# Weight tiles as three 256-column matmuls into one PSUM region, without the copy and add of result halves

## The chip, the cores and the metric

The kernel runs on one core of one Trainium2 chip. The metric is the device time of one execution in microseconds (us); lower is better. TensorE is called PE in the profile (PEld is its weight loads), VectorE DVE, ScalarE ACT, GpSimd POOL, SyncE SP.

## The reference, cut to what matters

Two layers over 256 tokens of width 2048, all in float32. Nearly all of the arithmetic is in products of a 256-row activation with a large weight matrix:

```python
for layer in range(2):
    hn = rms_norm(h, mix_norm[layer])
    if layer == 0:   # attention: 2048 -> 2560 (q, k, v), then 2048 -> 2048
        mix = swa_sink_attention(hn, a_w_qkv, a_b_qkv, a_sinks, a_w_o, a_b_o)
    else:            # recurrent block: 2048 -> 4096, gates, scan over time, 2048 -> 2048
        mix = rglru_block(hn, b_w_in, ..., b_w_out, b_b_out)
    h = h + mix
    h = h + jnp.square(jax.nn.relu(rms_norm(h, mlp_norm[layer]) @ w_up)) @ w_down   # 2048 -> 8192 -> 2048
return rms_norm(h, final_norm)
```

## The kernel before, in words

Everything is kept transposed: 128 features on the partitions and 256 tokens (TOK) along a row. To keep float32 accuracy, each operand is split into a rounded high part and the rest: a weight w becomes w_hi and w_lo, an activation becomes a pair stored as `operand[:, 0]` (high) and `operand[:, 1]` (low). A product is then hi·hi + hi·lo + lo·hi.

The weights are streamed in 85 "quads" of 512 output features: 5 for q, k, v; 4 for the attention's output; 32 for each MLP; 8 for the recurrent block's input; 4 for its output. A quad has two halves of 256 output features ("pairs"), a half has four chunks of four 128-row weight blocks, and a chunk has eight weight tiles of 128x128 (two output blocks b, four rows k). So a half has 32 tiles, a quad 64, the kernel 85·64 = 5440. A half writes two PSUM banks, and the two halves of a quad use different ones.

Each engine has its own program with the order of its work written out by hand:

- SP loads each 512 KB chunk into `w_raw`, which has eight slots; a slot is free once DVE has made w_lo from it.
- ACT makes w_hi from each chunk (`split_hi`, L343), as soon as the products of the chunk one half earlier have left that place. At the end of each half, between the third and fourth chunk's split, it runs `copy_half` (L356, or L359 and L360 with a bias added): it copies columns 256 to 511 of the two banks to `half` in SBUF.
- DVE makes w_lo (`split_lo`, L766). At the end of each half it runs `add_halves` (L780): u = bank columns 0 to 255 + half. What follows works on u: an addition to h (`residual`, L806, or `final_step`, L1225), ReLU and scaling (`up_step`, L1018, then squares at L1021 and the split at L1024), or scaling by rstd (`qkv_scale` L853, `scaled` L1136).
- PE runs `products`: per tile a matmul of w_hi with both parts of the activation, 512 columns wide (L1258), which puts hi·hi in columns 0 to 255 of a bank and hi·lo in columns 256 to 511, and then a matmul of w_lo with the high part, 256 columns, added to columns 256 to 511 (L1260). Before a half it waits until DVE has read the half before last from PSUM (`psum_free`). Each matmul instruction is preceded by its own weight load.
- The function `three` (L1277 to L1279) already exists in the kernel for smaller products: it adds hi·hi, hi·lo and lo·hi in one place with three matmuls. The attention scores, the attention output (both layer 0) and the gates of the recurrent block use it.

In the recurrent block's input stage each quad is one block n. Beside its chunks, ACT and DVE carry a convolution, gates, exponentials, a scan and a GeLU in a hand-written order (`lru_quad`), and PE runs 24 gate matmuls in each quad.

Of the kernel before, what the change touches and what calls it, by code (L numbers as in the profile page):

```python
# [28 lines left out]
TOK = 256  # L29
# [88 lines left out]
def build(nc, x_l, vec_d, const_d, w_qkv, w_o, w_in, ga_w, gx_w, w_out, w_up, w_down, out_l):  # L118
# [12 lines left out]
    with ctx:  # L131
# [13 lines left out]
        half = sb("half", [PART, 2, TOK])  # L145
# [66 lines left out]
        half_copied, psum_free = sem("half_copied"), sem("psum_free")  # L212
# [118 lines left out]
        def _(act):  # L331
# [16 lines left out]
            def copy_half(q, half_i, bias=None, done=None):  # L348


                act.wait_ge(wts_used, (q * 2 + half_i + 1) * CHUNKS if done is None else done)
                if not (isinstance(q, int) and q == 0 and half_i == 0):
                    act.wait_ge(psum_free, q * 2 + half_i)
                src = ps[:, 2 * half_i:2 * half_i + 2, TOK:2 * TOK]
                if bias is None:
                    nc.scalar.activation(half[:, :, :], src, ACT.Copy).then_inc(half_copied, 1)  # L356
                    return
                name, j = bias
                nc.scalar.activation(half[:, 0, :], src[:, 0, :], ACT.Identity, bias=col(name, j * 2))  # L359
                nc.scalar.activation(half[:, 1, :], src[:, 1, :], ACT.Identity,  # L360
                                     bias=col(name, j * 2 + 1)).then_inc(half_copied, 1)

# [25 lines left out]
            def residual(q, half_i, j, bias=None, norm=None, done=None):  # L388
                copy_half(q, half_i, bias, done)
# [4 lines left out]
            def late_residuals(q, bias, norm):  # L394

                copy_half(q, 0, (bias, 0), late_done(q))
# [3 lines left out]
                residual(q, 1, 1, (bias, 1), norm)  # L400
# [64 lines left out]
            copy_half(0, 0)  # L465
# [6 lines left out]
            copy_half(0, 1)  # L472
# [18 lines left out]
            copy_half(1, 0)  # L491
# [9 lines left out]
            copy_half(1, 1)  # L501
# [3 lines left out]
            def attention_step(q, half_i, j):  # L505


                next_hi(q, half_i, 0)
                pt_split_hi(j - 1)
                roped_hi(j)  # L510
                if half_i == 0:
                    act.wait_ge(v_read, 1)
                    vcur_split_hi(q - 2)
                next_hi(q, half_i, 1)
                next_hi(q, half_i, 2)
                softmax_exp(j, 0)
                softmax_exp(j, 1)
                copy_half(q, half_i)
                att_hi(j - 1)
                q_bias(j + 1)  # L520
                next_hi(q, half_i, 3)
# [22 lines left out]
            late_residuals(QB_WO, "b_o", (1, "mlp0"))  # L544

            def residual_step(q, half_i, j, bias=None, norm=None):
                for s in range(3):
                    next_hi(q, half_i, s)
                residual(q, half_i, j, bias, norm)
                next_hi(q, half_i, 3)  # L550

            with act.Fori(1, Q_WO) as i:
                residual_step(i + QB_WO, 0, i * 2, ("b_o", i * 2), (1, "mlp0"))
                residual_step(i + QB_WO, 1, i * 2 + 1, ("b_o", i * 2 + 1), (1, "mlp0"))


            def up_step(q, half_i, j, relus, norm=None):

                for s in range(3):
                    next_hi(q, half_i, s)  # L560
                if norm is not None:
                    root(norm)
                copy_half(q, half_i)
# [27 lines left out]
            with act.Fori(0, 4) as i:  # L591
                residual_step(i + last, 0, i * 2, None, (2, "mix1"))
                residual_step(i + last, 1, i * 2 + 1, None, (2, "mix1"))
# [69 lines left out]
            def lru_quad(q, n, before, recur):  # L663
# [21 lines left out]
                copy_half(q, 0)  # L685
# [10 lines left out]
                copy_half(q, 1)  # L696
# [23 lines left out]
            late_residuals(q, "b_out", (3, "mlp1"))  # L720
            with act.Fori(1, Q_WO) as i:
                residual_step(i + QB_OUT, 0, i * 2, ("b_out", i * 2), (3, "mlp1"))
                residual_step(i + QB_OUT, 1, i * 2 + 1, ("b_out", i * 2 + 1), (3, "mlp1"))
# [4 lines left out]
            def final_step(q, half_i, j, more=True):  # L728
# [3 lines left out]
                copy_half(q, half_i)  # L732
# [21 lines left out]
        def _(dve):  # L754
# [49 lines left out]
            def residual(q, half_i, j, norm=None):  # L804
                add_halves(q, half_i)
                add = nc.vector.tensor_tensor(h_pair(j), h_pair(j), u[:, :, :], ALU.add)  # L806
# [5 lines left out]
            def residual_step(q, half_i, j, norm=None):  # L812
                for s in range(3):
                    next_lo(q, half_i, s)
                residual(q, half_i, j, norm)
                next_lo(q, half_i, 3)

            def late_residuals(q, norm):
                add_halves(q, 0)
                nc.vector.tensor_tensor(h_pair(0), h_pair(0), u[:, :, :], ALU.add).then_inc(h_ready, 1)  # L820
# [3 lines left out]
                residual(q, 1, 1, norm)  # L824
# [24 lines left out]
            def qkv_scale(q, half_i, added=False):  # L849

                if not added:
                    add_halves(q, half_i)
                nc.vector.tensor_tensor(u[:, :, :], u[:, :, :], bc2(rstd[:, :]), ALU.mult).then_inc(qkv_scaled, 1)  # L853
# [64 lines left out]
            add_halves(0, 0)  # L918
# [5 lines left out]
            qkv_scale(0, 0, added=True)  # L924
# [79 lines left out]
            late_residuals(QB_WO, (1, "mlp0"))  # L1004
            dve.wait_ge(x_again_rest, 16)
            with dve.Fori(1, Q_WO) as i:
                residual_step(i + QB_WO, 0, i * 2, (1, "mlp0"))
                residual_step(i + QB_WO, 1, i * 2 + 1, (1, "mlp0"))


            def up_step(q, half_i, j, relus, norm=None):
# [3 lines left out]
                if norm is not None:  # L1015
                    inverse_root(norm)
                add_halves(q, half_i)
# [34 lines left out]
            with dve.Fori(0, 4) as i:  # L1052
                residual_step(i + last, 0, i * 2, (2, "mix1"))
                residual_step(i + last, 1, i * 2 + 1, (2, "mix1"))
# [78 lines left out]
            def scaled(q, half_i):  # L1133

                add_halves(q, half_i)
                return nc.vector.tensor_tensor(u[:, :, :], u[:, :, :], bc2(rstd[:, :]), ALU.mult)  # L1136
# [18 lines left out]
            def lru_quad(q, n, before, recur):  # L1155
# [23 lines left out]
                scaled(q, 0).then_inc(x_scaled, 1)  # L1179
# [8 lines left out]
                scaled(q, 1).then_inc(y_scaled, 1)  # L1188
# [24 lines left out]
            late_residuals(q, (3, "mlp1"))  # L1213
            with dve.Fori(1, Q_WO) as i:
                residual_step(i + QB_OUT, 0, i * 2, (3, "mlp1"))
                residual_step(i + QB_OUT, 1, i * 2 + 1, (3, "mlp1"))
# [3 lines left out]
            def final_step(q, half_i, j, more=True):  # L1220
# [3 lines left out]
                add_halves(q, half_i)  # L1224
                nc.vector.tensor_tensor(h_pair(j), h_pair(j), u[:, :, :], ALU.add).then_inc(h_ready, 1)  # L1225
# [19 lines left out]
        def _(pe):  # L1245
            def products(q, half_i, s, operand, ready_sem, ready, late=False):
# [27 lines left out]

            def three(out, hi_w, lo_w, hi_x, lo_x, first, last):

                nc.tensor.matmul(out, hi_w, hi_x, start=first, stop=False)  # L1277
                nc.tensor.matmul(out, hi_w, lo_x, start=False, stop=False)  # L1278
                return nc.tensor.matmul(out, lo_w, hi_x, start=False, stop=last)  # L1279
# [207 lines left out]
```

## Time and profile before

| what | value |
|---|---|
| median of the runs | 2039.28 us (2 runs: 2038.20 and 2040.36) |
| span of the profiled execution, first to last instruction | 2025.1 us |
| median less span (launch and end, outside the trace) | 14.2 us |
| granted TensorE clock, mean | 0.995 of 2.4 GHz |
| PE busy | 99% of the span |
| PEld busy | 87% |
| DVE busy, ACT busy | 67%, 52% |
| mean traffic to memory | 182 GB/s |

The span is the time that the trace can account for. No total of the profiled execution is given beside its span, so the span is set against the median of the two runs. Matmul ends are modelled and matmuls overlap, so for PE it is the distance from one start to the next that tells the pace, not the length of one.

### The profile page before, as it was taken

The numbers are of one execution on the slowest core, as the hardware profiler recorded it, in microseconds if no ns is written. First come the engines' busy times: TensorE is split into PE (matmuls) and PEld (weight loads), VectorE is DVE, ScalarE is ACT, GpSimd is POOL, SyncE is SP. The second block draws the span as 40 slices with busy tenths as digits, with TensorE's granted clock in tenths as the row PEclk, the third lists the DMA queues.
The fourth block names the chain that finished last, engine by engine and source line by source line (L and its number), as shares of the span: only waits on it lengthen the run. The fifth ranks groups of instructions, "written<-read, shape, count | busy, mean of one in ns | idle before, by whom it ended". The sixth has DMA issues, their size and how long they took to land.

```text
span 2025.1 us, 34220 instructions
## 1 busy us (share of the span) xinstructions
PE 1995.1 (99%) x11604; PEld 1756.6 (87%) x11604; DVE 1361.0 (67%) x1560; ACT 1056.6 (52%) x1437; POOL 8.7 (0%) x12
## 2 busy tenths in 40 slices
PE   9999999999999999999999999999999999999997
PEld 8888888888888888888888888888888888888886
DVE  7777676656655665666788897676566556656665
ACT  7555554444444444445588885554444444444453
POOL 1000000000000000000000000000000000000000
PEclk9999999999999999999999999999999999999999
DMA  8433656656565655655556554565656566565652
GB/s 276 141 104 115 196 167 207 191 185 195 178 202 179 198 188 186 195 178 190 194 177 183 180 176 159 194 193 188 191 179 198 193 186 189 186 195 177 199 175 92
DMA packets 365879, 368.12 MB, mean 182 GB/s; under 512 B 11536, under 2 KB 363920, under 8 KB 365712
## 3 DMA queue, kind: packets, MB, share of 16 engines
q1 hardware_dynamic: 365552, 365.53, 57.0%
q0 software_dynamic: 288, 2.10, 0.3%
q8 instruction: 22, 0.36, 0.1%
q14 instruction: 17, 0.14, 0.0%
HBM read 365.48 MB, written 2.10 MB: 182 GB/s over the span
## 4 chain that ended last, share of the span: by engine, by line
PE 88%; DVE 5%; ACT 4%; issue 2%; DMA 0%; ACTq 0%; DVEq 0%; SPq 0%
PE ps L1258 55%; PE ps L1260 29%; DVE w_lo L766 1%; ACT w_hi L343 1%; PE aux L1277 1%; PE aux L1278 1%; PE aux L1279 1%; DVE u L780 1%; DVE u L1136 0%; DVE v L1100 0%; ACT L634 0%; ACT L614 0%; PE aux L1293 0%; PE aux L1330 0%; DMA h<-x_l_dram 0%
## 5 line engine op out<-in xcount | busy, mean ns | idle before, releaser
L766 DVE TENSOR_TENSOR w_lo<-w_raw,w_hi 128x1024 fp32r<-128x1024 f32 x678 | 817.4, 1223 | 338.0 <-ACT w_hi L343 337.0
L1258 PE MATMUL ps<-xn,w_hi 128*128 128x512 f32 x2880 | 1007.8, 394 | 7.4 <-DVE w_lo L766 5.0
L343 ACT ACTIVATE w_hi<-w_raw 128x1024 fp32r<-128x1024 f32 x678 | 701.3, 1053 | 432.5 <-PE ps L1260 429.6
L1258 PE MATMUL ps<-mid,w_hi 128*128 128x512 f32 x2544 | 888.2, 393 | 5.4 <-DVE mid L1124 3.0
L1260 PE MATMUL ps<-xn,w_lo 128*128 128x256 f32 x2880 | 808.1, 281 | 0.0
L1260 PE MATMUL ps<-mid,w_lo 128*128 128x256 f32 x2544 | 713.7, 281 | 0.0
L1258 PEld LDWEIGHTS ps<-xn,w_hi 128*128 128x128 f32 x2880 | 540.3, 188 | 128.2 <-issue 9.0
L1258 PEld LDWEIGHTS ps<-mid,w_hi 128*128 128x128 f32 x2544 | 477.0, 188 | 113.2 <-issue 5.1
L1260 PEld LDWEIGHTS ps<-xn,w_lo 128*128 128x128 f32 x2880 | 546.4, 190 | 0.6 <-issue 0.5
L1260 PEld LDWEIGHTS ps<-mid,w_lo 128*128 128x128 f32 x2544 | 482.2, 190 | 0.2 <-issue 0.2
L780 DVE TENSOR_TENSOR u<-ps,half 128x512 f32<-128x512 f32 x170 | 117.5, 691 | 183.2 <-ACT half L356 161.1
L356 ACT ACTIVATE half<-ps 128x512 f32<-128x512 f32 x154 | 91.8, 596 | 227.1 <-PE ps L1260 227.1
L565 ACT ACTIVATE mid<-u 128x512 f32 (+1 forms) x64 | 40.6, 634 | 105.4 <-DVE u L1018 105.4
L1024 DVE TENSOR_TENSOR mid<-v,mid 128x512 f32 (+1 forms) x64 | 44.3, 693 | 22.9 <-ACT mid L565 22.8
L806 DVE TENSOR_TENSOR h<-h,u 128x512 f32 (+1 forms) x70 | 48.5, 693 | 11.6 <-DVE u L780 11.5
L796 DVE SCALAR_TENSOR_TENSOR xn<-h,vec,xn (+1 forms) x48 | 21.2, 482 | 40.3 <-ACT xn L378 40.3
L1021 DVE TENSOR_TENSOR v<-u 128x512 f32<-128x512 f32 x64 | 44.4, 693 | 2.2
L1018 DVE SCALAR_TENSOR_TENSOR u<-u,rstd 128x512 f32<-128x512 f32 x64 | 44.3, 692 | 2.2
L376 ACT ACTIVATE sq<-h 128x512 f32 (+1 forms) x24 | 15.2, 633 | 40.1 <-DVE h L806 38.9
L785 DVE TENSOR_TENSOR acc<-acc,sq 128x512 f32<-128x512 f32 x31 | 21.3, 687 | 5.8 <-ACT sq L735 5.8
L1143 DVE SCALAR_TENSOR_TENSOR xc<-xb,vec,xc 128x256 f32<-128x256 f32 x48 | 21.1, 482 | 3.5 <-ACT xc L655 1.5
L359 ACT ACTIVATE half<-ps,vec 128x256 f32<-128x256 f32 x16 | 7.5, 472 | 29.3 <-PE ps L1260 29.3
(152 smaller groups left out, 807.0 us busy)
## 6 DMA issues: line engine op xcount, KB each, us to landing
w_raw<-mlp_w_up_dram SPq DMA_DIRECT2D x256, 512.0 KB, 3.8
w_raw<-mlp_w_down_dram SPq DMA_DIRECT2D x256, 512.0 KB, 3.5
w_raw<-b_w_in_dram SPq DMA_DIRECT2D x64, 512.0 KB, 3.9
w_raw<-a_w_qkv_dram SPq DMA_DIRECT2D x40, 512.0 KB, 5.3
w_raw<-a_w_o_dram SPq DMA_DIRECT2D x32, 512.0 KB, 3.5
w_raw<-b_w_out_dram SPq DMA_DIRECT2D x32, 512.0 KB, 4.1
h<-x_l_dram SPq DMA_DIRECT2D x4, 512.0 KB, 8.6
gate_raw<-b_gate_a_w_dram SPq DMA_DIRECT2D x8, 256.0 KB, 3.9
```

The costliest lines, as they stand in the source:

```text
L343: nc.scalar.activation(w_hi[:, s, :, :], w_raw[:, slot, :, :], ACT.Copy).then_inc(hi_ready, 1)
L356: nc.scalar.activation(half[:, :, :], src, ACT.Copy).then_inc(half_copied, 1)
L565: nc.scalar.activation(mid[:, 0, bass.ds(j * 2, 2), :], u[:, :, :], ACT.Square).then_inc(mid_hi, 1)
L766: nc.vector.tensor_tensor(w_lo[:, s, :, :], w_raw[:, slot, :, :], w_hi[:, s, :, :].bitcast(F32), ALU.subtract).then_inc(lo_ready, 1)
L780: nc.vector.tensor_tensor(u[:, :, :], ps[:, 2 * half_i:2 * half_i + 2, 0:TOK], half[:, :, :], ALU.add).then_inc(psum_free, 1)
L785: return nc.vector.tensor_tensor(acc[:, :, :], acc[:, :, :], sq[:, :, :], ALU.add)
L806: add = nc.vector.tensor_tensor(h_pair(j), h_pair(j), u[:, :, :], ALU.add)
L1018: nc.vector.scalar_tensor_tensor(u[:, :, :], in0=u[:, :, :], scalar=0.0, in1=bc2(rstd[:, :]), op0=ALU.max, op1=ALU.mult).then_inc(relu_rea ...
L1021: nc.vector.tensor_tensor(v[:, :, :], u[:, :, :], u[:, :, :], ALU.mult).then_inc(squared, 1)
L1024: nc.vector.tensor_tensor(mid[:, 1, bass.ds(j * 2, 2), :], v[:, :, :], mid[:, 0, bass.ds(j * 2, 2), :].bitcast(F32), ALU.subtract).then_in ...
L1258: nc.tensor.matmul(bank[:, :], hi[:, k, cols], operand[:, :, kt, :], start=kt == 0, stop=False)
L1260: last = nc.tensor.matmul(bank[:, TOK:2 * TOK], lo[:, k, cols], operand[:, 0, kt, :], start=False, stop=kt == KT - 1)
```

## The change

`products` uses `three` for each weight tile: w_hi with the high part of the activation, w_hi with the low part, w_lo with the high part, each 256 columns, all added in columns 0 to 255 of the bank. Columns 256 to 511 are no longer used. `half`, `copy_half` and `add_halves` go. DVE's next operation reads the bank directly and signals `psum_free` itself; it then waits for that signal and raises the semaphore of the result with an instruction of its own. Where ACT added a bias during the copy (the two output projections), DVE now adds it in two operations of 256 columns that compute h = (bank + bias) + h.

```diff
-            def copy_half(q, half_i, bias=None, done=None):
-                act.wait_ge(wts_used, (q * 2 + half_i + 1) * CHUNKS if done is None else done)
-                if not (isinstance(q, int) and q == 0 and half_i == 0):
-                    act.wait_ge(psum_free, q * 2 + half_i)
-                src = ps[:, 2 * half_i:2 * half_i + 2, TOK:2 * TOK]
-                if bias is None:
-                    nc.scalar.activation(half[:, :, :], src, ACT.Copy).then_inc(half_copied, 1)
-                    return
...
-            def add_halves(q, half_i):
-                dve.wait_ge(half_copied, q * 2 + half_i + 1)
-                nc.vector.tensor_tensor(u[:, :, :], ps[:, 2 * half_i:2 * half_i + 2, 0:TOK], half[:, :, :],
-                                        ALU.add).then_inc(psum_free, 1)
-                dve.wait_ge(psum_free, q * 2 + half_i + 1)
+            def sums(q, half_i, done=None):
+                dve.wait_ge(wts_used, (q * 2 + half_i + 1) * CHUNKS if done is None else done)
+                return ps[:, 2 * half_i:2 * half_i + 2, 0:TOK]
...
+            def residual(q, half_i, j, bias=None, norm=None, done=None):
+                src = sums(q, half_i, done)
+                if bias is None:
+                    nc.vector.tensor_tensor(h_pair(j), h_pair(j), src, ALU.add).then_inc(psum_free, 1)
+                else:
+                    for b in range(2):
+                        one = h[:, bass.ds(j * 2 + b, 1), :]
+                        add = nc.vector.scalar_tensor_tensor(one, in0=src[:, b:b + 1, :], scalar=col(bias, j * 2 + b),
+                                                             in1=one, op0=ALU.add, op1=ALU.add)
+                    add.then_inc(psum_free, 1)
                 if norm is not None:
                     n, gain = norm
-                    add.then_inc(h_ready, 1)
+                    dve.wait_ge(psum_free, q * 2 + half_i + 1)
+                    dve.sem_inc(h_ready, 1)
                     norm_operand(j, j + (8 * (n - 1) + 1), gain)
...
             def up_step(q, half_i, j, relus, norm=None):
...
-                add_halves(q, half_i)
-                nc.vector.scalar_tensor_tensor(u[:, :, :], in0=u[:, :, :], scalar=0.0, in1=bc2(rstd[:, :]),
-                                               op0=ALU.max, op1=ALU.mult).then_inc(relu_ready, 1)
-                dve.wait_ge(relu_ready, relus + 1)
+                nc.vector.scalar_tensor_tensor(u[:, :, :], in0=sums(q, half_i), scalar=0.0, in1=bc2(rstd[:, :]),
+                                               op0=ALU.max, op1=ALU.mult).then_inc(psum_free, 1)
+                dve.wait_ge(psum_free, q * 2 + half_i + 1)
+                dve.sem_inc(relu_ready, 1)
...
+            def scaled(q, half_i, ready):
+                nc.vector.tensor_tensor(u[:, :, :], sums(q, half_i), bc2(rstd[:, :]), ALU.mult
+                                        ).then_inc(psum_free, 1)
+                dve.wait_ge(psum_free, q * 2 + half_i + 1)
+                dve.sem_inc(ready, 1)
...
             def products(q, half_i, s, operand, ready_sem, ready, late=False):
...
-                        nc.tensor.matmul(bank[:, :], hi[:, k, cols], operand[:, :, kt, :],
-                                         start=kt == 0, stop=False)
-                        last = nc.tensor.matmul(bank[:, TOK:2 * TOK], lo[:, k, cols], operand[:, 0, kt, :],
-                                                start=False, stop=kt == KT - 1)
+                        last = three(bank[:, 0:TOK], hi[:, k, cols], lo[:, k, cols], operand[:, 0, kt, :],
+                                     operand[:, 1, kt, :], kt == 0, kt == KT - 1)
```

## Rows read from the trace of the kernel before

**Rows 1.** The page: busy times, and the chain that ended last by engine

```profile
PE 1995.1 (99%) x11604; PEld 1756.6 (87%) x11604; DVE 1361.0 (67%) x1560; ACT 1056.6 (52%) x1437; POOL 8.7 (0%) x12
PE 88%; DVE 5%; ACT 4%; issue 2%; DMA 0%; ACTq 0%; DVEq 0%; SPq 0%
```

**Rows 2.** Waits: engine and line, whom it waited for, us, times, longest

```profile
ACT w_hi L343 <- PE ps L1260: 429.6, 305, 1.7
DVE w_lo L766 <- ACT w_hi L343: 337.0, 330, 5.0
```

**Rows 3.** Groups by line and form: count, busy us, mean ns, idle before

```profile
L1258 PE MATMUL ps<-xn,w_hi 128*128 128x512 f32 x2880 | 1007.8, 394 | 7.4 <-DVE w_lo L766 5.0 <-DVE xn L834 2.4
L1258 PE MATMUL ps<-mid,w_hi 128*128 128x512 f32 x2544 | 888.2, 393 | 5.4 <-DVE mid L1124 3.0 <-DVE mid L903 1.5 <-DVE w_lo L766 0.9
...
L1260 PEld LDWEIGHTS ps<-xn,w_lo 128*128 128x128 f32 x2880 | 546.4, 190 | 0.6 <-issue 0.5
...
L780 DVE TENSOR_TENSOR u<-ps,half 128x512 f32<-128x512 f32 x170 | 117.5, 691 | 183.2 <-ACT half L356 161.1 <-ACT half L360 21.9
L356 ACT ACTIVATE half<-ps 128x512 f32<-128x512 f32 x154 | 91.8, 596 | 227.1 <-PE ps L1260 227.1
```

**Rows 4.** Busy time by stretch: us, busy and count of each engine, PEclk

```profile
20.00:210.00 190.00, 184.68 (x1173) 161.98 (x1172) 142.98 (x196) 109.37 (x254) 2.58 (x3) 1.00 0.46 146
...
300.00:1016.00 716.00, 716.00 (x4131) 631.45 (x4130) 458.25 (x499) 336.78 (x388) 0.00 (x0) 1.00 0.60 188
...
1100.00:1205.00 105.00, 101.56 (x612) 89.93 (x611) 93.58 (x125) 89.90 (x132) 0.00 (x0) 1.00 0.57 176
```

**Rows 5.** PE's timeline in an MLP stage: start us, length us, what

```profile
599.90 0.39 PE L1258 MATMUL ps<-mid,w_hi 128*128 128x512 f32 x1
600.13 0.28 PE L1260 MATMUL ps<-mid,w_lo 128*128 128x256 f32 x1
600.25 0.39 PE L1258 MATMUL ps<-mid,w_hi 128*128 128x512 f32 x1
...
609.26 0.39 PE L1258 MATMUL ps<-mid,w_hi 128*128 128x512 f32 x1
```

**Rows 6.** The same view, the 24 gate matmuls of one quad

```profile
1023.75 0.28 PE L1277 MATMUL aux<-xc_split,gate_hi 128*128 128x256 f32 x1
1023.87 0.28 PE L1278 MATMUL aux<-xc_split,gate_hi 128*128 128x256 f32 x1
...
1026.14 0.28 PE L1279 MATMUL aux<-xc_split,gate_lo 128*128 128x256 f32 x1
```

**Rows 7.** The same view, attention scores (256 columns), then attention output (128)

```profile
151.96 0.29 PE L1278 MATMUL aux<-kpad,qz 128*128 x1
...
154.60 0.28 PE L1279 MATMUL aux<-kpad,qz 128*128 x1
...
154.78 0.28 PE L1278 MATMUL aux<-pt,vcur 128*128 128x128 f32 x1
...
157.24 0.28 PE L1279 MATMUL aux<-pt,vcur 128*128 128x128 f32 x1
```

**Rows 8.** Waits between 1070 and 1202 us, in the recurrent block's input stage

```profile
PE ps L1258 <- DVE w_lo L766: 3.9, 5, 0.9
```

**Rows 9.** PE's timeline at single stalls

```profile
1018.97 0.47 PE L1258 MATMUL ps<-xn,w_hi 128*128 128x512 f32 x1 [1.84 <-DVE w_lo L766]
...
1122.65 0.47 PE L1258 MATMUL ps<-xn,w_hi 128*128 128x512 f32 x1 [0.90 <-DVE w_lo L766]
...
1148.89 0.47 PE L1258 MATMUL ps<-xn,w_hi 128*128 128x512 f32 x1 [0.90 <-DVE w_lo L766]
...
1224.55 0.51 PE L1258 MATMUL ps<-mid,w_hi 128*128 128x512 f32 x1 [2.97 <-DVE mid L1124]
```

**Rows 10.** Timeline of the end, behind the last product

```profile
2011.50 0.69 DVE L780 TENSOR_TENSOR u<-ps,half 128x512 f32<-128x512 f32 x1 [5.85 <-ACT half L356]
2012.22 0.69 DVE L1225 TENSOR_TENSOR h<-h,u 128x512 f32<-128x512 f32 x1
```

More of the change, by code:

```diff
@@ L211, in build @@
         hi_ready, lo_ready, wts_used = sem("hi_ready"), sem("lo_ready"), sem("wts_used")
-        half_copied, psum_free = sem("half_copied"), sem("psum_free")
+        psum_free = sem("psum_free")
         h_ready, xn_hi, xn_ready = sem("h_ready"), sem("xn_hi"), sem("xn_ready")
@@ L386, in root, with residual @@
                                      ).then_inc(rms_ready, 1)
-            def residual(q, half_i, j, bias=None, norm=None, done=None):
-                copy_half(q, half_i, bias, done)
+            def residual(j, norm=None):
                 if norm is not None:
@@ L392, in residual, with late_residuals @@
                     norm_operand(j, j + (8 * (n - 1) + 1), gain)
-            def late_residuals(q, bias, norm):
-                copy_half(q, 0, (bias, 0), late_done(q))
+            def late_residuals(q, norm):
                 after_late_hi(q, 3)
@@ L399, in late_residuals @@
                 norm_operand(0, 8 * (n - 1) + 1, gain)
-                residual(q, 1, 1, (bias, 1), norm)
+                residual(1, norm)
             act.wait_ge(consts_set, 2)
@@ L471, in _ @@
             root(0)
-            copy_half(0, 1)
             next_hi(0, 1, 3)
@@ L591, in _ @@
             with act.Fori(0, 4) as i:
-                residual_step(i + last, 0, i * 2, None, (2, "mix1"))
-                residual_step(i + last, 1, i * 2 + 1, None, (2, "mix1"))
+                residual_step(i + last, 0, i * 2, (2, "mix1"))
+                residual_step(i + last, 1, i * 2 + 1, (2, "mix1"))
             def gate_sigmoids(n):
@@ L802, in norm_operand, with residual_step, late_residuals @@
                 sum_squares().then_inc(acc_ready, 1)
[L804 to L806 removed]
+            def residual(q, half_i, j, bias=None, norm=None, done=None):
[8 more added lines that the diff above has]
+                    add.then_inc(psum_free, 1)
                 if norm is not None:
                     n, gain = norm
[L809 removed]
+                    dve.wait_ge(psum_free, q * 2 + half_i + 1)
+                    dve.sem_inc(h_ready, 1)
                     norm_operand(j, j + (8 * (n - 1) + 1), gain)
[L812 removed]
+            def residual_step(q, half_i, j, bias=None, norm=None):
                 for s in range(3):
                     next_lo(q, half_i, s)
[L815 removed]
+                residual(q, half_i, j, bias, norm)
                 next_lo(q, half_i, 3)
[L818 to L820 removed]
+            def late_residuals(q, bias, norm):
+                residual(q, 0, 0, bias, None, late_done(q))
+                dve.wait_ge(psum_free, q * 2 + 1)
+                dve.sem_inc(h_ready, 1)
                 next_lo(q, 1, 3)
@@ L823, in late_residuals @@
                 norm_operand(0, 8 * (n - 1) + 1, gain)
-                residual(q, 1, 1, norm)
+                residual(q, 1, 1, bias, norm)
             then(nc.vector.memset(acc[:, :, :], 0.0))
@@ L1052, in _ @@
             with dve.Fori(0, 4) as i:
-                residual_step(i + last, 0, i * 2, (2, "mix1"))
-                residual_step(i + last, 1, i * 2 + 1, (2, "mix1"))
+                residual_step(i + last, 0, i * 2, None, (2, "mix1"))
+                residual_step(i + last, 1, i * 2 + 1, None, (2, "mix1"))
             def softplus_of_minus_lambda():
@@ L1223, in final_step @@
                         next_lo(q, half_i, s)
-                add_halves(q, half_i)
-                nc.vector.tensor_tensor(h_pair(j), h_pair(j), u[:, :, :], ALU.add).then_inc(h_ready, 1)
+                residual(q, half_i, j)
+                dve.wait_ge(psum_free, q * 2 + half_i + 1)
+                dve.sem_inc(h_ready, 1)
                 if more:
@@ L1245, in _, with three @@
         def _(pe):
+            def three(out, hi_w, lo_w, hi_x, lo_x, first, last):
+                nc.tensor.matmul(out, hi_w, hi_x, start=first, stop=False)
+                nc.tensor.matmul(out, hi_w, lo_x, start=False, stop=False)
+                return nc.tensor.matmul(out, lo_w, hi_x, start=False, stop=last)
             def products(q, half_i, s, operand, ready_sem, ready, late=False):
@@ L1273, in quad @@
                 pair(q, 1, operand, ready_sem, ready, between_b)
[L1275 to L1279, printed above, removed]
             def stats(n):
```

61 lines of the change are left out of this document (22 added, 39 removed).

## The prediction

> **What bounds the kernel now.** I read the busy shares and the chain of waits first. PE is busy 99% of the span and makes 88% of the chain; DVE and ACT are busy 67% and 52% [rows 1]. The largest waits all point the same way: ACT waited 429.6 us for PE to leave a weight place and DVE 337.0 us for ACT [rows 2], while PE's own idle time in its main lines is 7.4 and 5.4 us [rows 3]. So the pace of the products is the pace of the kernel, and the question is whether it is set by columns, by instructions, or by weight loads. In an MLP stage, 28 tiles start between 599.90 and 609.26 us: 9.36 us over 27 steps is 346.7 ns a tile, 0.23 us after the wide matmul and 0.12 us after the narrow one [rows 5]. Over 716 us, 4131 matmuls make 2065.5 tiles, again 346.6 ns each, with PE never idle and the clock at its upper level of 2.4 GHz [rows 4]. 768 columns at 2.4 GHz are 320 ns, so 26.7 ns a tile, 13.3 ns a matmul, is a cost that goes with instructions and not with columns.
>
> **The tile with three matmuls.** The trace of before already holds this form. In the gates, 20 steps from 1023.75 to 1026.14 us take 2.39 us: 119.5 ns a matmul of 256 columns [rows 6]. In the attention scores 22 steps from 151.96 to 154.60 us take 2.64 us: 120.0 ns [rows 7]. 256 columns are 106.7 ns, so the rest is 12.8 to 13.3 ns, the same cost per matmul as in the pair above. The two readings support each other: the columns stay 768, and one more matmul costs one more such piece. With 119.75 ns, the middle, a tile takes 359.25 ns against 346.65, so 12.6 ns more. There are 5440 tiles (5424 of their wide matmuls are in two rows of [rows 3]): 5440 x 12.6 ns = **+68.5 us**. By the two ends, 358.5 and 360.0 ns, it is +64 to +73 us. The step after a narrow matmul that is followed by a wide one is 0.115 to 0.12 us [rows 5]; three steps of 0.116 would be 348 ns and +7 us. That is the lower bound for this term, and I stay near the rows that have three narrow ones in a row.
>
> Each matmul loads its own weights, w_hi now twice. A load is recorded at 190 ns [rows 3], longer than the step of 120 ns, but in the gates loads and matmuls keep that step 24 times over, and with 128 columns the step still falls to 111.8 ns (22 steps from 154.78 to 157.24 us, [rows 7]). So a load with its matmul can follow at 112 ns, and 120 ns is above that floor, though by 8 ns only.
>
> The Trainium skill ("TensorE: Matmul & The Clock Gate", LDWEIGHTS) estimates a weight load of 128 columns at 107 ns; the floor of 111.8 ns in [rows 7] agrees roughly. The same page (Back-to-back issue gap) gives an isolated gap of N/2.4 + 2.5 ns. By that rule the third matmul would add 2.5 ns a tile, +13.6 us in all; the 13 ns of rows 5 to 7 don't agree.
>
> **The copy and the addition that go.** Per half, ACT saves a copy of 596 ns and DVE an addition of 691 ns [rows 3]. There are 170 halves, so DVE loses 117.5 us of work and ACT about 100 us. Almost all of it is beside PE: in an MLP stage DVE is busy 458.25 of 716 us and ACT 336.78 [rows 4], and PE doesn't wait there. A reader of PSUM still follows at the end of each half, and the next writer of those banks comes a half (11 us) later, so `psum_free` isn't late in either kernel. The new wait of DVE for its own operation, plus the instruction that raises the semaphore, replaces the same kind of wait behind the addition. I take it at nothing; at 0.1 us each it is covered by DVE's idle third, and if the cover were gone it would be 17 us. The bias, moved from ACT into two 256-column operations on DVE, concerns 16 halves and lies in stages where DVE has the same slack.
>
> The removed work is on the path in five places:
>
> - Recurrent input stage. PE waits for w_lo five times between 1070 and 1202 us, 3.9 us of idle [rows 8]. The distance between two such stalls, 1122.65 to 1148.89 us, is 26.24 us a quad [rows 9]. PE alone needs 64 x 0.3467 + 24 x 0.1195 = 25.06 us, so here the exchange between ACT and DVE sets the pace, DVE being 89% busy [rows 4]. After the change that exchange is shorter by two copies and two additions at most (2.6 us), so 23.7 to 25.5 us, while PE needs 64 x 0.3593 + 2.87 = 25.9 us. PE takes over and the stalls go: -3.9 us, and about 0.16 us at each restart, **-4.7 us**. Nothing if the exchange doesn't get shorter.
> - First quad of that stage: one stall of 1.84 us [rows 9] behind a chain on DVE with one copy and addition in it. Between 0 and -1.3 us; I take **-1.0 us**.
> - The stall of 2.97 us before the last chunk of the recurrent output [rows 9] waits for DVE's recurrence. Seven chunks of eight tiles on PE take 0.7 us more in the meantime: **-0.7 us**, at most -2 us.
> - Attention stage: between 20 and 210 us PE is idle for 190.0 - 184.7 = 5.3 us [rows 4], which I read as its waits for the chain from the result of one half to the scores of the next, a chain that begins with the copy and addition. I take a little over a quarter, **-1.5 us**, between 0 and -4 us.
> - The end: the copy ends just before 2011.50, DVE adds the halves, then h at 2012.22 us, and ACT's squares wait for that [rows 10]. The addition with its gap (0.72 us) and the copy (0.6 us) go: **-1.3 us**.
>
> Sum: 68.5 - 4.7 - 1.0 - 0.7 - 1.5 - 1.3 = +59.3 us. The profiled span is 2025.1 us and becomes 2084.4; with the 14.2 us that lie around it in the median, the time is 2098.6 us, say **2098 us**. Bounds of the parts together: 64 - 13 = +51 to 73 - 4 = +69 us, plus 17 us if the semaphore step were uncovered.
>
> **Rivals.**
>
> 1. *A third narrow matmul costs much less than the rows say.* If the fixed part goes with the wide matmul (its step is 0.23 us) or with the change of weights, a repeated w_hi may be nearly free. Three steps of 0.116 us make +7 us, less the 9.2 us saved: 2037 us, not slower. It decides below a step of 118.6 ns in the products, where the change stays within 41 us, and below 116.1 ns nothing is lost at all. For it: the narrow step in [rows 5] is at the low end. Against it: in the gates the second matmul also has the weights of the first, and its steps are not shorter [rows 6]. The page's 2.5 ns gives +13.6 - 9.2, 2044 us. Chance 0.10 for this side as a whole.
> 2. *The weight loads become the bound.* If the loads can't keep 120 ns for thousands of matmuls in a row, where the rows show it for 24, or for the scores and the output right behind them, the tile grows. One load after the other at 190 ns would be 570 ns a tile and +1215 us, 3245 us; a slip of only 5 ns a matmul is +82 us more, 2180 us. Against it: steps of 111.8 ns exist [rows 7], and the pace of the pair holds over 716 us [rows 4]. Chance 0.06, nearly all at its low end. The same page of the Trainium skill (What overlaps and what doesn't) says a load overlaps running matmuls only when the row group differs; by that a tile would be far slower, and the loads of 128 rows hidden in [rows 6] don't agree.
> 3. *ACT and DVE were holding PE more than I count.* Then removing 220 us of their work would give more than 9 us back. PE's idle is 2025.1 - 1995.1 = 30 us over the whole span [rows 1], of which some 14 are start and end, so at most 16 us come back: 68.5 - 17 gives 2091 us. This is inside the forecast's own range.
>
> **How the numbers follow.** Forecast 0.84 with rival 3 in it, rival 1 0.10, rival 2 0.06. A measurement of this kernel can tell about 2%, 41 us, from no change; slower by over 2% begins at 2080 us. The forecast's bounds, 2090 to 2108 us, lie above it, and rival 2 too; rival 1 lies within 2%, and I leave 0.02 for a gain that I don't see. Slower 0.87, same 0.11, faster 0.02. The range reaches from 2080 us (fixed cost a third smaller than read) to 2114 us (the semaphore step uncovered in part).
>
> **What would show it right or wrong.** In the profile after: steps of 0.12 us between all three matmuls of a tile, 359 ns a tile and 11.5 us a half; PE still at 99% and three times 5440 matmuls; PEld busy above 87%; DVE busy down to some 1245 us and ACT to about 957 us. The stalls for w_lo between 1070 and 1202 us are gone and a quad there takes 25.9 us. Steps at 0.116 us in the products would make rival 1 right, steps of 0.125 us or more rival 2. If the span grows by less than 50 us with steps of 0.12 us, my list of places where the copy was on the path is too short.

## The result, and the profile after

The changed kernel took 2080.89 us (2 runs: 2080.28 and 2081.50) against 2039.28 us: 1.020 times the time of before, with a 95% interval of 1.0138 to 1.0262. A second comparison on one chip gave 1.0201 (1.0153 to 1.0249). It is slower, by 41.6 us: no change lies outside the interval, but whether the loss is above or below 2% stays open. The prediction was 2098 us, in a range of 2080 to 2114 us.

The profiled execution has a span of 2079.6 us and a time of 2081.50 us, so 1.9 us lie outside the span. That is already a surprise: the prediction had put 14.2 us there.

The page's busy times and its chain by engine, after (before: [rows 1]):

```profile
PE 2058.8 (99%) x17044; PEld 2050.5 (99%) x17044; DVE 1260.4 (61%) x1406; ACT 969.0 (47%) x1251; POOL 8.7 (0%) x12
PE 96%; DVE 2%; ACT 1%; issue 0%; DMA 0%; DVEq 0%; SPq 0%; ACTq 0%
```

PE has 5440 matmuls more, as counted, and still sets the end; its share of the chain rose from 88% to 96%. The weight loads went from 87% to 99% busy. DVE lost 100.6 us of work and ACT 87.6 us, and most of that doesn't show in the time.

PE's timeline in an MLP stage, after (before: [rows 5]); columns are start, length, what:

```profile
600.05 0.28 PE L1231 MATMUL ps<-mid,w_hi 128*128 128x256 f32 x1
600.17 0.28 PE L1232 MATMUL ps<-mid,w_hi 128*128 128x256 f32 x1
600.29 0.28 PE L1233 MATMUL ps<-mid,w_lo 128*128 128x256 f32 x1
600.41 0.28 PE L1231 MATMUL ps<-mid,w_hi 128*128 128x256 f32 x1
```

Every step is 0.12 us, whether the next matmul has the same weights (L1231 to L1232) or others. The busy time by stretch, after (before: [rows 4]); us, busy and count of PE, PEld, DVE, ACT, POOL, then the clock:

```profile
20.00:210.00 190.00, 186.45 (x1511) 180.02 (x1509) 135.12 (x183) 103.02 (x243) 2.04 (x2) 1.00 0.46 145
300.00:1016.00 716.00, 716.00 (x5969) 716.00 (x5969) 400.02 (x395) 287.52 (x302) 0.00 (x0) 1.00 0.59 182
1100.00:1205.00 105.00, 105.00 (x879) 105.00 (x878) 90.37 (x118) 87.02 (x126) 0.00 (x0) 1.00 0.59 181
```

716 us over 5969 / 3 tiles is 359.9 ns a tile, against 346.6 ns. In the recurrent stage (the last row) PE was idle 3.4 us of 105 before and isn't idle any more. The single stalls and the end, after (before: [rows 9, 10]):

```profile
1050.30 0.35 PE L1231 MATMUL ps<-xn,w_hi 128*128 128x256 f32 x1 [1.04 <-DVE w_lo L739]
...
1253.63 0.36 PE L1231 MATMUL ps<-mid,w_hi 128*128 128x256 f32 x1 [1.77 <-DVE mid L1104]
...
2066.43 0.28 PE L1233 MATMUL ps<-mid,w_lo 128*128 128x256 f32 x1
...
2066.74 0.69 DVE L778 TENSOR_TENSOR h<-h,ps 128x512 f32<-128x512 f32 x1 [6.96 <-PE ps L1233]
2067.52 0.63 ACT L708 ACTIVATE sq<-h 128x512 f32<-128x512 f32 x1 [8.90 <-DVEq L1208]
```

The stalls of 1.84 and 2.97 us are now 1.04 and 1.77 us, and behind the last product there is one DVE operation where there were a copy and two additions.

Two more things are needed for the account below: the last product of before, and the clock behind the two single stalls. First the row of before:

```profile
2010.55 0.28 PE L1260 MATMUL ps<-mid,w_lo 128*128 128x256 f32 x1
```

Then the stretches behind the two stalls and at 211 us; columns are the stretch, its length, PE's busy time and count, and then the clock. Before:

```profile
209.00:212.00 3.00, 2.83 (x16) 1.00 0.56 134
1020.00:1023.00 3.00, 3.00 (x11) 0.51 0.77 208
1225.00:1228.00 3.00, 3.00 (x11) 0.50 0.41 120
```

and after:

```profile
211.00:214.00 3.00, 3.00 (x16) 0.50 0.54 168
1052.00:1055.00 3.00, 3.00 (x27) 1.00 0.84 255
1255.00:1258.00 3.00, 3.00 (x28) 1.00 0.68 215
```

So the spans differ by 2079.6 - 2025.1 = 54.5 us and the times by 41.6 us. The change can't have cost both; the experiments had to find where 13 us went.

### The profile page after: what moved, and what is told of

It is laid out like the page before. It is cut to its first block, busy times and chain, and to the rows that moved or that the text cites. A ratio compares the mean times of both kernels' runs of the same rounds, so it can differ in the third digit from the quotient of the medians.

```text
span 2079.6 us, 44579 instructions
## 1 busy us (share of the span) xinstructions
PE 2058.8 (99%) x17044; PEld 2050.5 (99%) x17044; DVE 1260.4 (61%) x1406; ACT 969.0 (47%) x1251; POOL 8.7 (0%) x12
## 4 chain that ended last, share of the span: by engine, by line
PE 96%; DVE 2%; ACT 1%; issue 0%; DMA 0%; DVEq 0%; SPq 0%; ACTq 0%
PE ps L1231 31%; PE ps L1232 31%; PE ps L1233 31%; PE aux L1231 1%; PE aux L1232 1%; PE aux L1233 1%; PE aux L1274 0%; PE aux L1311 0%; DMA h<-x_l_dram 0%; DVE qz L853 0%; DVE h L1224 0%; DVE w_lo L739 0%; ACT pt L412 0%; ACT w_hi L342 0%; DVE xc L1125 0%
## 5 line engine op out<-in xcount | busy, mean ns | idle before, releaser
L342 ACT ACTIVATE w_hi<-w_raw 128x1024 fp32r<-128x1024 f32 x678 | 710.9, 1055 | 724.1 <-PE ps L1233 720.1
L1231 PE MATMUL ps<-xn,w_hi 128*128 128x256 f32 x2880 | 818.2, 284 | 4.0 <-DVE xn L814 1.7
L1232 PE MATMUL ps<-xn,w_hi 128*128 128x256 f32 x2880 | 815.5, 283 | 0.0
L1231 PE MATMUL ps<-mid,w_hi 128*128 128x256 f32 x2544 | 721.3, 284 | 3.3 <-DVE mid L1104 1.8
L1232 PE MATMUL ps<-mid,w_hi 128*128 128x256 f32 x2544 | 720.6, 283 | 0.0
L1231 PEld LDWEIGHTS ps<-xn,w_hi 128*128 128x128 f32 x2880 | 553.4, 192 | 5.1 <-issue 5.0
L1232 PEld LDWEIGHTS ps<-xn,w_hi 128*128 128x128 f32 x2880 | 553.3, 192 | 0.6 <-issue 0.5
L1231 PEld LDWEIGHTS ps<-mid,w_hi 128*128 128x128 f32 x2544 | 489.1, 192 | 3.8 <-issue 3.8
L1232 PEld LDWEIGHTS ps<-mid,w_hi 128*128 128x128 f32 x2544 | 489.0, 192 | 0.2 <-issue 0.2
L1233 PEld LDWEIGHTS ps<-mid,w_lo 128*128 128x128 f32 x2544 | 489.1, 192 | 0.0
L778 DVE TENSOR_TENSOR h<-h,ps 128x512 f32 (+1 forms) x64 | 44.0, 687 | 50.8 <-PE ps L1233 50.8
L997 DVE SCALAR_TENSOR_TENSOR u<-ps,rstd 128x512 f32<-128x512 f32 x64 | 44.3, 692 | 35.0 <-PE ps L1233 34.9
```

The lines of the kernel that those rows point to most:

```text
L342: nc.scalar.activation(w_hi[:, s, :, :], w_raw[:, slot, :, :], ACT.Copy).then_inc(hi_ready, 1)
L778: nc.vector.tensor_tensor(h_pair(j), h_pair(j), src, ALU.add).then_inc(psum_free, 1)
L997: nc.vector.scalar_tensor_tensor(u[:, :, :], in0=sums(q, half_i), scalar=0.0, in1=bc2(rstd[:, :]), op0=ALU.max, op1=ALU.mult).then_inc(psu ...
```

## The experiments

**The change once more, and its two halves apart.** `after_again` is the changed kernel.

> The changed kernel once more, against the kernel before on the same chip. Theory A (each matmul costs its columns at 2.4 GHz and 13.3 ns more): tiles at 360 ns against 347, +71 us, less 17 us of stalls and end, so the span grows by 54 us. The single comparison gave +54.5 us in the spans but +41.6 us in the times. If both are the growth of one quantity, the time grows by 54 us here too (ratio 1.027); if something outside the span or between executions took 13 us of it, the ratio is 1.020 again.

It took 2080.75 us; its 6 executions lie between 2078.28 and 2081.80 us. The kernel before, 17 times on the same chip, had a median of 2040.30 us but spread over three levels: six executions from 2025.19 to 2030.50 us, seven from 2038.28 to 2042.49, four from 2050.82 to 2055.54, some 13 us apart. The changed kernel has one. So the ratio is repeatable at 1.020, and the trace of before that the prediction read, with its span of 2025.1 us, belongs to the lowest level.

`three_with_halves` takes three matmuls but keeps the two halves of a bank, the copy and the addition:

```diff
-                        nc.tensor.matmul(bank[:, :], hi[:, k, cols], operand[:, :, kt, :],
-                                         start=kt == 0, stop=False)
+                        if kt == 0:
+                            nc.tensor.matmul(bank[:, :], hi[:, k, cols], operand[:, :, kt, :],
+                                             start=True, stop=False)
+                        else:
+                            nc.tensor.matmul(bank[:, 0:TOK], hi[:, k, cols], operand[:, 0, kt, :],
+                                             start=False, stop=False)
+                            nc.tensor.matmul(bank[:, TOK:2 * TOK], hi[:, k, cols], operand[:, 1, kt, :],
+                                             start=False, stop=False)
```

> The kernel before with three matmuls of 256 columns a tile, but in the places of before (hi hi in the left half, hi lo and lo hi in the right), so the copy and the addition stay. The first tile of each bank, 340 of 5440, keeps the wide matmul. Theory A: the cost is the count of matmuls, 5100 x 13.2 ns = +67 us over before, and about 12 us over the changed kernel. Theory B (the cost is adding three times into one place): about the time of before. Theory C (copy and addition matter little): equal to the changed kernel plus a few us.

It took 2080.96 us, 0.2 us from the changed kernel in the same comparison. Its first MLP:

```profile
300.00:1000.00 700.00, 700.00 (x5730) 1.00 0.58 182
```

A bank has 16 tiles, here with 15 x 3 + 2 = 47 matmuls, so this is 700 x 47 / (5730 x 16) = 358.9 ns a tile; fifteen tiles at 360 and one at 346.6 ns would be 359.2. Theory B falls: adding into one place costs nothing by itself, the count of matmuls does all of it. Theory A is right on that and wrong on the 12 us; the time is the one that theory C named. Its 340 wide tiles save 340 x 13.3 ns = 4.5 us, so the copy and addition cost about 5 us here, where PE is the slower partner.

`wide_without_copy` is the other half: DVE and ACT of the changed kernel, PE of the kernel before.

```diff
-                        last = three(bank[:, 0:TOK], hi[:, k, cols], lo[:, k, cols], operand[:, 0, kt, :],
-                                     operand[:, 1, kt, :], kt == 0, kt == KT - 1)
+                        nc.tensor.matmul(bank[:, :], hi[:, k, cols], operand[:, :, kt, :],
+                                         start=kt == 0, stop=False)
+                        last = nc.tensor.matmul(bank[:, 0:TOK], lo[:, k, cols], operand[:, 0, kt, :],
+                                                start=False, stop=kt == KT - 1)
```

> The changed kernel with the wide matmul of before: w_hi 512 columns wide, w_lo into the left half, and DVE reads the left half alone. It leaves out the product of w_hi with the low part of the activation. Theory A: tiles at 347 ns and the stalls and the end of the changed kernel, 9 to 17 us below the kernel before (2022 to 2030 us). Theory C: the copy and addition were hidden, within 3 us of before.

2028.57 us (0.9957 of before, 0.9921 to 0.9993): as theory A expected, at the upper part of its range. Eleven of its 12 executions lie between 2027.08 and 2029.82 us, one at 2043.41 us. Its trace told more. The busy time of PE by stretch in `wide_without_copy`, the first MLP and the second:

```profile
300.00:1000.00 700.00, 700.00 (x4040) 1.00 0.60 190
1330.00:2000.00 670.00, 670.00 (x3794) 1.00 0.58 182
```

With PE never idle and the clock at 2.4 GHz in both, a tile takes 700 / 2020 = 346.5 ns in one stretch and 670 / 1897 = 353.2 ns in the other. The same instructions have two paces.

**Two more traces of the kernel before.**

> The kernel before, unchanged, for its trace. Its times on one chip lie near 2026, 2040 and 2054 us, 14 us apart. Theory D (the wide and narrow pair has two paces, 346.7 and 353.3 ns a tile, and keeps one from one stall of PE to the next; wide_without_copy ran its first MLP at 346.7 and its second at 353.3): an execution of 2040 us has one of the two long stretches (210 to 1016 us, 1225 to 2011 us) at 353.3 ns, one of 2054 has both, one of 2026 neither, and the span is 2 us below the time. Theory E (time outside the span, 14 us): all traces have a span near 2025 us and 346.7 ns throughout.

> As before_1: a second draw. Theory D: time 2026, 2040 or 2054 us with 0, 1 or 2 long stretches at 353.3 ns a tile. Theory E: span near 2025 us whatever the time.

`before_1` took 2051.76 us with a span of 2049.8, `before_2` 2038.74 us with a span of 2036.8. The same two stretches in `before_1`:

```profile
300.00:1000.00 700.00, 700.00 (x3964) 1.00 0.59 186
1330.00:2000.00 670.00, 670.00 (x3795) 1.00 0.59 186
```

and in `before_2`:

```profile
300.00:1000.00 700.00, 700.00 (x3965) 1.00 0.59 186
1330.00:2000.00 670.00, 670.00 (x3867) 1.00 0.60 189
```

Read the counts: 3964 matmuls in 700 us are 353.2 ns a tile, 3867 in 670 us are 346.5 ns. `before_1` has both stretches slow, `before_2` the first alone, and the trace that the prediction read neither (4041 in the first). A long stretch has some 2040 tiles, and 2040 x 6.7 ns is 13.7 us, the distance between the levels. Theory D holds, theory E falls: in every execution whose time and span are both known, 2 us lie outside the span.

Where does the pace change? PE's timeline around the sum-of-squares matmuls (L1284, L1285) at the start of the first MLP, in `before_1`:

```profile
293.92 0.28 PE L1260 MATMUL ps<-xn,w_lo 128*128 128x256 f32 x1
294.04 0.59 PE L1284 MATMUL aux<-acc,ones 128*128 128x256 f32 x2
294.47 0.59 PE L1285 MATMUL aux<-acc,ones 128*128 128x256 f32 x2
...
295.60 0.40 PE L1258 MATMUL ps<-xn,w_hi 128*128 128x512 f32 x1
295.83 0.28 PE L1260 MATMUL ps<-xn,w_lo 128*128 128x256 f32 x1
295.95 0.40 PE L1258 MATMUL ps<-xn,w_hi 128*128 128x512 f32 x1
```

The wide matmul is recorded at 0.40 us where the fast pace has 0.39 [rows 5]. The starts over 700 us say the same: the step behind a wide matmul is 230.2 ns in the first trace and 236.4 in `before_1`, the step behind a narrow one 116.4 and 117.0 ns, so nearly all of the slow pace sits in the wide one. The stretch ahead of this point ran at the fast pace here, and at the slow one in the trace of [rows 5]; both flipped at L1285. The matmul counts in the 70 us before and the 700 us after that point are 398 and 4041 in the first trace, 406 and 3964 in `before_1`, 407 and 3965 in `before_2`. The second MLP's start flips in the same manner in these three traces, but not in `wide_without_copy` (slow before and after).

**What a matmul costs.** `equal_384` has the same columns and the same count as before, in equal parts:

```diff
+                        x = operand[:, 0, kt - kt % 2:kt - kt % 2 + 2, 0:192]
+                        nc.tensor.matmul(bank[:, 0:384], hi[:, k, cols], x, start=False, stop=False)
+                        last = nc.tensor.matmul(bank[:, 128:512], lo[:, k, cols], x,
+                                                start=False, stop=kt == KT - 1)
```

> The kernel before with the same 768 columns in two matmuls of 384 each (both read the high part of the activation of two row blocks, so the products are others than the reference's; the first tile of each bank is as before). Theory A (columns and a fixed piece per matmul): 346.7 ns a tile, the time of before or its lower level, 2026 to 2040 us. Theory F (a wide matmul is cheap and a narrow one dear, so only the width matters, not the count): another pace than 346.7 ns, by more than 3 ns a tile or 16 us.

It took 2023.09 us, 4 executions within 2021.82 to 2024.43 us. Its first MLP:

```profile
300.00:1000.00 700.00, 700.00 (x4040) 1.00 0.60 190
```

That is 346.5 ns a tile, as theory A says, though the time is 3 us below the 2026 us where its range began. Neither width is dear or cheap for itself: a step is 120 ns with 256 columns and 173.3 with 384, both 13.3 ns over the columns at 2.4 GHz. This form has shown one pace only.

`four_192` splits the 768 columns into four:

```diff
+                        x = operand[:, 0, kt, 0:192]
+                        for n, (side, at) in enumerate(((hi, 0), (hi, 192), (lo, 320), (lo, 64))):
+                            last = nc.tensor.matmul(bank[:, at:at + 192], side[:, k, cols], x,
+                                                    start=False, stop=kt == KT - 1 and n == 3)
```

> The same 768 columns a tile in four matmuls of 192 (w_hi, w_hi, w_lo, w_lo; they don't form the reference's products; the first tile of each bank is as before). Theory A without a floor: 4 x (80 + 13.3) = 373 ns a tile, about +145 us over the fast pace, 2170 us. With the floor of 111.8 ns that the 128-column matmuls of the attention show (one weight load each): 4 x 112 = 447 ns, +550 us, 2575 us.

2511.35 us. The stretch of the first MLP in `four_192`:

```profile
300.00:1000.00 700.00, 700.00 (x6158) 695.88 (x6157) 347.07 (x358) 253.94 (x286) 0.00 (x0) 1.00 0.48 149
```

700 / 6158 is 113.7 ns a matmul, not 93. This mean has in it the first tile of each bank, which still is a wide and a narrow matmul. Inside a bank:

```profile
1500.96 0.39 PE L1266 MATMUL ps<-mid,w_hi 128*128 128x192 f32 x2
...
1503.64 0.39 PE L1266 MATMUL ps<-mid,w_hi 128*128 128x192 f32 x2
```

Between these starts lie 24 matmuls in 2.68 us, 111.7 ns each. That is the floor of 111.8 ns that the prediction read from matmuls of 128 columns [rows 7]: with its own weight load, 192 columns take no longer than 128. The three matmuls of the change, at 120 ns, are just above it: the next narrower form would no longer pay for columns alone. The time is 64 us under the 2575 us expected, mostly because that sum charged all 5440 tiles and not the 5100 that were changed (34 us), and because PE's idle time fell by 14 us.

**Other orders, to be rid of the slow pace.** `paired_order` alternates by twos (wide, narrow, narrow, wide), `grouped_8` and `grouped_4` run eight or four wide matmuls and then as many narrow ones. In `paired_order`:

```diff
+                    for k in range(0, CH_KT, 2):
+                        wide(k)
+                        narrow(k)
+                        narrow(k + 1)
+                        last = wide(k + 1)
```

> The kernel before with the order of the matmuls in two tiles as wide, narrow, narrow, wide, so that the regular alternation is broken; same instructions and sums. Theory D: the second pace may no longer exist; if the pace is 346.7 ns throughout, the time is 2026 us in every execution, 14 us below the median of before. If the slow pace stays, 2026 to 2054 us as before. Theory A alone says nothing of a second pace: 2026 us.

> The kernel before with the same matmuls in another order: in each chunk the eight wide ones first, then the eight narrow ones. Theory D with the second pace bound to the alternation of widths: runs of equal widths have one pace each, 226.7 ns wide and 120 ns narrow, 346.7 ns a tile throughout, 2026 us in every execution, 14 us below the median of before. If the second pace belongs to a width and not to the alternation, 2026 to 2054 us in steps of 14.

> As grouped_8, but four wide and four narrow matmuls in turn, twice the changes of width. Theory D as for grouped_8: 2026 us. If each change of width costs a little, between grouped_8 and paired_order (2031 us).

| kernel | time, us | executions | against before (95%) | matmuls in 300 to 1000 us | ns a tile |
|---|---|---|---|---|---|
| paired_order | 2030.57 | 12, 2027.98 to 2034.28 | 0.995 (0.9922 to 0.9978) | 4021 | 348.2 |
| grouped_8 | 2034.70 | 12, 2034.16 to 2038.91 | 0.9992 (0.9966 to 1.0017) | 4013 | 348.9 |
| grouped_4 | 2042.76 | 10, 2040.68 to 2044.03 | 1.0029 (1.0000 to 1.0059) | 3993 | 350.6 |

All three are free of the levels, and none reaches 346.7 ns. The expectation that runs of equal width have their pace to themselves failed. In `grouped_8`, where the view merges equal matmuls in a row:

```profile
599.99 2.00 PE L1255 MATMUL ps<-mid,w_hi 128*128 128x512 f32 x8
601.83 1.12 PE L1258 MATMUL ps<-mid,w_lo 128*128 128x256 f32 x8
602.78 2.00 PE L1255 MATMUL ps<-mid,w_hi 128*128 128x512 f32 x8
```

Eight wide steps take 1.84 us, 230 ns each, and eight narrow ones 0.95 us, 118.8 ns each. Averaged over 700 us, the first five wide steps of a run are 228 to 236 ns and the last three 226.7, which is the columns and 13.3 ns again; the first narrow step is 113.3 ns, from the third on it is 120.0. So wide matmuls behind narrow ones pay for a while, and narrow ones behind wide ones gain a little less. It isn't a price for each change of width: fours change width twice as often as eights and are dearer, but twos and strict alternation change it more often still and are cheaper. `grouped_4` at 2042.76 us is above the 2031 to 2035 us that such a price would have given. Of the kernels that form the reference's products, `paired_order` alone has a median under that of before, by half a per cent; the lowest level of before, 2026 us, is still faster.

**What sets the pace of a stretch.** Two kernels change what PE does in the half after the sum-of-squares matmuls, 32 tiles of some 2040, and leave the rest. `split_after_stats` splits 30 of that half's 32 wide matmuls:

```diff
-                quad(base, *operand, {3: lambda: stats(norm)})
+                pair(base, 0, *operand, {3: lambda: stats(norm)})
+                pair(base, 1, *operand, split=True)
```

`wide_run_after_stats` orders that half's last chunk, eight tiles, as eight narrow and then eight wide matmuls.

> The kernel before, but in the half that follows the sum-of-squares matmuls at the start of each MLP, each wide matmul is two of 256 columns, in the same places (60 of 64 tiles, twice 30 x 13 ns, under 1 us). In the traces so far the pace of a stretch changes at those sum-of-squares matmuls, at 294 and at 1311 to 1322 us. Theory D1 (what PE does just before a stretch of pairs decides its pace): now every stretch starts from even steps of 120 ns and the times no longer spread in steps of 14 us; 2027 us if it enters the fast pace, 2055 us if the slow one. Theory D2 (the pace is drawn by something else): 2027, 2041 and 2055 us as before.

> As split_after_stats, but the last chunk of that half runs its eight narrow matmuls first and its eight wide ones last, so each long stretch of pairs is entered from eight wide matmuls in a row. Theory D1 (what PE does just before a stretch decides its pace): the times no longer spread in steps of 14 us; both stretches at 346.7 ns and 2027 us, 12 us under the median of before, or both at 353.3 ns and 2055 us. Theory D2: 2027, 2041 and 2055 us as before.

2051.23 us (6 executions, 2050.89 to 2056.21; 1.0085 of before, 1.0053 to 1.0116) and 2052.58 us (12 executions, 2050.13 to 2056.47; 1.0054, 1.0029 to 1.0079). In `wide_run_after_stats`:

```profile
300.00:1000.00 700.00, 700.00 (x3965) 1.00 0.59 186
1330.00:2000.00 670.00, 670.00 (x3795) 1.00 0.59 185
```

Both stretches are slow in the trace, and the twelve times lie at the upper level. The trace shows the flip itself, first ahead of the reordered chunk and then behind it:

```profile
296.99 0.39 PE L1268 MATMUL ps<-xn,w_hi 128*128 128x512 f32 x1
...
304.61 0.39 PE L1268 MATMUL ps<-xn,w_hi 128*128 128x512 f32 x1
...
304.96 1.11 PE L1256 MATMUL ps<-xn,w_lo 128*128 128x256 f32 x8
305.91 2.00 PE L1259 MATMUL ps<-xn,w_hi 128*128 128x512 f32 x8
...
308.09 0.40 PE L1268 MATMUL ps<-xn,w_hi 128*128 128x512 f32 x1
...
315.86 0.40 PE L1268 MATMUL ps<-xn,w_hi 128*128 128x512 f32 x1
```

From 296.99 to 304.61 us there are 22 tiles at 346.4 ns, and from 308.09 to 315.86 us 22 tiles at 353.2 ns. The sum-of-squares matmuls had left the pairs at the fast pace, and the reordered chunk turned them to the slow one. D1 holds as far as it goes: what PE runs just ahead decides the pace of 700 us of unchanged work. Neither way in gave the fast pace for the long stretch, and a way that does so every time was not found.

## Why the prediction was right or wrong

*The third matmul.* Right in kind and nearly in size. The tile went from 346.6 to 359.9 ns, +13.3 ns where 12.6 was taken: +72 us for +68.5. The working by columns plus a fixed piece, and the reading of the form in the gates and the scores [rows 6, 7], carried the forecast. Rival 1 falls: a repeated w_hi costs a full step. The Trainium skill ("TensorE: Matmul & The Clock Gate", Back-to-back issue gap) gives a gap of N/2.4 + 2.5 ns for an isolated matmul. The trace doesn't agree, as the fixed piece is 13.3 ns here.

*The weight loads.* Rival 2 falls too. PEld is 99% busy and the step holds 120 ns over 716 us. The same page of the Trainium skill (What overlaps and what doesn't) says that a load overlaps running matmuls only in another row group. That isn't borne out: 5969 loads of all 128 rows stood beside 5969 matmuls in that stretch. The floor is real, though, and `four_192` shows it at 111.7 ns.

*The copy and addition.* Between the two traces 72 - 54.5, some 18 us, came back, where 9.3 was forecast. Three things make up most of it.

The first is PE's idle time, and here the forecast was nearly right. It fell from 2025.1 - 1995.1 = 30.0 us to 2079.6 - 2058.8 = 20.8 us, by 9.2 us. In the recurrent stage PE has no wait for w_lo left (3.9 us), and a quad takes 25.9 us as forecast (the gate matmuls of a quad start at 1053.24 us, those of the seventh after it at 1234.45). The two single stalls lost 0.8 and 1.2 us, the end 1.3 us, and the wait before the first products 0.7 us, which wasn't in the list. The attention's idle time went from 5.3 to 4.3 us: the window from 20 to 210 us shows 190.0 - 186.45 = 3.55 us, but 0.7 us of its last stall lies behind 210 us. From the start of the last product to the end of the span it is 2025.1 - 2010.55 = 14.5 us before and 2079.6 - 2066.43 = 13.2 us after.

The second, which the sum left out, is the clock behind the stalls. Behind the stalls of 1.84 and 2.97 us the trace of before was granted 0.51 and 0.50, the lower level of 1.2 GHz, for some 3 us; the tiles there took about 0.64 us. Behind the shorter stalls of after it was granted 1.00. Each such dip costs about 1.5 us, five tiles at 0.64 and not 0.35 us. The trace of after has one at 211 us in return, behind a stall of 1.50 us that had no dip behind it in the first trace. So one dip, 1.5 us, came back on balance.

The third is that not all of the trace of before ran at 346.6 ns a tile. The stretches just ahead of the two MLPs ran at 353 ns (398 and 407 matmuls in 70 us are the two paces), and so did parts of the attention stage. Over all tiles without a stall the starts give a mean of 347.6 ns before and 359.9 ns after, so the tiles cost about 67 us more and not 72. These three come to some 16 us; the last 2 us were not assigned.

How much is the copy's own doing? `three_with_halves`, which keeps it, has 2079.2 - 2054.3 = 24.9 us of idle time: 5.1 of the 9.2 us went with the copy still there, because PE got slower and the others caught up. Beside the wide matmuls the copy is worth more: `before_2` and `wide_without_copy`, with one long slow stretch each, have spans of 2036.8 and 2026.7 us. Rival 3 allowed for up to 16 us of idle time; 9.2 us came back. The semaphore step, taken at nothing, held: PE is never idle in 716 us of MLP.

*The time around the span.* This is the step that failed: "with the 14.2 us that lie around it in the median". 2 us lie there. The other 12 were the slow pace in one of the two long stretches. The two executions of before that gave the median, at 2038.20 and 2040.36 us, left no trace; that they had one slow stretch is concluded from their times, which are those of the middle level and of `before_2`. The profiled one had none. The changed kernel pays 360 ns a tile whichever it was, so against a median with one slow stretch it loses 13.7 us less. 2025.1 + 59.3 + 2 would have been 2086 us. A second pace wasn't among the rivals; two times 13 and 15 us above the span were there to be asked about.

So the direction and the mechanism held, and the range only just: 2080.89 us is 0.9 us above its lower edge. That is luck. The edge was set for a fixed cost a third smaller (by the prediction's own terms that gives 2098.6 - 68.5 / 3 = 2076 us, not 2080), while the fixed cost was as read and the base was wrong. The 17 us between 2098 and 2081 us are 12 us of a base wrongly read and 5 us of net over-count in the terms.

## What to carry to other kernels

If weights are loaded anew for each matmul, count a matmul as its columns at 2.4 GHz and about 13 ns, and not under 112 ns: one wide moving operand is cheaper than two narrow ones on the same weights, and what the narrow form spares on the other engines is worth little while PE is the bound (here 188 us of their work for 5 us of time). Before a prediction takes a trace as the base, set its span against the spread of the times; 2 us lay between them in all runs here, and a gap well above that meant that the trace wasn't the median execution. And read a pace from counts in a long busy stretch: "100% busy" was said of 346.5 and of 353.2 ns alike.

## What the runs showed that was not expected

- A regular alternation of 512- and 256-column matmuls runs at 346.5 or 353.2 ns a pair, keeps its pace for 700 us and more, and can take the other one at the float32 matmuls of the sum of squares or at one reordered chunk. Levels of about 2026, 2040 and 2053 us in the kernel before come from that. Equal widths (3 x 256, 2 x 384) showed one pace each: 359.9 and 346.5 ns. The cause inside PE stays open.
- 60 tiles of 5440, split at the entries of the two stretches, moved the median of the whole kernel from 2038 to 2051 us, and 16 tiles that were only reordered there moved it from 2039 to 2053 us.
- The order of the widths has a price of its own, and it doesn't follow the number of changes: with the same matmuls, 346.5 ns a tile at best in strict alternation, 348.2 by twos, 350.6 by fours, 348.9 by eights.
- Weight load and matmul together showed no steady step under 112 ns, at 128 columns as at 192.
